# TensorE multiplies a constant block into an unread bank in eleven of its longer waits

## The reference: what is computed

```
mod = silu(c) @ w_ada + b_ada                      # shift, scale and gate of the two halves
mix = token_mixer(x * (1 + sc1) + sh1)             # w_in, sparse attention, a convolution, w_out
x   = layer_norm(ALPHA * x + g1 * mix)
ff  = (silu(h @ w_gate) * (h @ w_up)) @ w_down     # h = x * (1 + sc2) + sh2
x   = layer_norm(ALPHA * x + g2 * ff)
```

```
h = h + mixer(rms_norm(h))                         # w_in, recurrence or attention, w_out
h = h + swiglu(rms_norm(h))                        # 2816 hidden columns
h = h + sigmoid(rms_norm(h) @ w_gate) * (p @ w_proj)
```

## Time and profile before

| | us |
|---|---|
| median of 3 runs | 1235.39 (1232.58 to 1235.83) |
| the profiled execution, its own time | 1238.56 |
| its span, first to last instruction | 1236.7 |
| TensorE busy | 1087.3 (88%) |
| VectorE busy | 761.6 (62%) |
| ScalarE busy | 574.1 (46%) |
| GpSimd busy | 265.9 (21%) |
| mean granted TensorE clock | 0.926 |

### The profile page before, as it was taken

How to read it: one execution, slowest core, us unless ns; L and a number is a source line. 1 busy time by engine, 2 the same in 40 slices (tenths; PEclk the granted TensorE clock), 3 DMA queues, 4 the chain that set the end, 5 groups by cost and what they waited for, 6 DMA issues and landing times.

```text
span 1236.7 us, 20753 instructions
## 1 busy us (share of the span) xinstructions
PE 1087.3 (88%) x8097; PEld 1018.7 (82%) x8097; DVE 761.6 (62%) x1172; ACT 574.1 (46%) x963; POOL 265.9 (21%) x257
## 2 busy tenths in 40 slices
PE   1796646879999996989899999998998699999998
PEld 1786534869999985878799999998886499999997
DVE  5747876656655445775475665557676676555554
ACT  0544333455544335552364454465554655444452
POOL 0433232013332003020023332003120013333001
PEclk9897755889999998989899999998999899999999
DMA  8655453516553724341046554663334046553660
GB/s 314 212 203 185 156 203 136 168 37 206 202 182 113 216 75 173 132 173 68 1 162 210 174 180 141 187 235 140 137 136 136 1 137 204 203 169 110 196 207 36
DMA packets 188324, 193.45 MB, mean 156 GB/s; under 512 B 13721, under 2 KB 150722, under 8 KB 188130
## 3 DMA queue, kind: packets, MB, share of 16 engines
q1 hardware_dynamic: 184016, 179.88, 43.8%
q0 software_dynamic: 2640, 10.49, 2.3%
q10 hardware_dynamic: 1602, 2.18, 0.5%
HBM read 191.48 MB, written 1.05 MB: 156 GB/s over the span
## 4 chain that ended last, share of the span: by engine, by line
PE 66%; DVE 18%; ACT 6%; DMA 4%; issue 3%; POOL 1%; ACTq 1%; SPq 0%; POOLq 0%; DVEq 0%
PE gemm L1701 19%; PE gemm L1703 19%; PE gemm L1702 19%; DVE wlo L1152 5%; DMA raw<-in_w_in 3%; ACT whi L816 2%; DVE macc L1205 2%; PE aux L2013 1%; PE aux L1930 1%; DVE olo L1174 1%; DVE om L1423 1%; DVE xlo L1174 1%; DMA raw<-in_gla_w_in 1%; DMA raw<-in_w_ada 1%; DVE neg_max L1660 1%
## 5 line engine op out<-in xcount | busy, mean ns | idle before, releaser
L1701 PE MATMUL gemm<-ohi,whi 128*128 128x256 f32 x1536 | 442.2, 288 | 32.9 <-DVE wlo L1152 19.3
L1152 DVE TENSOR_TENSOR wlo<-raw,whi 128x1024 fp32r<-128x1024 f32 (+2 forms) x348 | 397.4, 1188 | 114.5 <-ACT whi L816 114.1
L1703 PE MATMUL gemm<-ohi,wlo 128*128 128x256 f32 x1536 | 437.0, 285 | 0.0
L1702 PE MATMUL gemm<-olo,whi 128*128 128x256 f32 x1536 | 436.4, 284 | 0.0
L816 ACT ACTIVATE whi<-raw 128x1024 fp32r<-128x1024 f32 (+2 forms) x348 | 309.2, 954 | 127.3 <-PE gemm L1703 100.8
L1701 PEld LDWEIGHTS gemm<-ohi,whi 128*128 128x128 f32 x1536 | 296.8, 193 | 40.4 <-DVE wlo L1152 22.3
L1702 PEld LDWEIGHTS gemm<-olo,whi 128*128 128x128 f32 x1536 | 297.4, 194 | 0.2
L1703 PEld LDWEIGHTS gemm<-ohi,wlo 128*128 128x128 f32 x1536 | 296.9, 193 | 0.0
L1701 PE MATMUL gemm<-acthi,whi 128*128 128x256 f32 x528 | 147.9, 280 | 0.0
L1703 PE MATMUL gemm<-acthi,wlo 128*128 128x256 f32 x528 | 147.6, 280 | 0.0
L1702 PE MATMUL gemm<-actlo,whi 128*128 128x256 f32 x528 | 147.3, 279 | 0.0
(11 more groups left out here) (306 smaller groups left out, 1488.2 us busy)
## 6 DMA issues: line engine op xcount, KB each, us to landing
raw<-in_ffn_w_in SPq DMA_DIRECT2D x44, 1024.0 KB, 6.8
raw<-in_ffn_w_out SPq DMA_DIRECT2D x32, 704.0 KB, 5.7
raw<-in_gla_w_in SPq DMA_DIRECT2D x6, 2048.0 KB, 7.8
raw<-in_diff_w_in SPq DMA_DIRECT2D x6, 2048.0 KB, 7.6
raw<-in_w_gate SPq DMA_DIRECT2D x11, 1024.0 KB, 5.1
raw<-in_w_up SPq DMA_DIRECT2D x11, 1024.0 KB, 7.5
raw<-in_w_down SPq DMA_DIRECT2D x16, 704.0 KB, 5.4
raw<-in_w_ada SPq DMA_DIRECT2D x5, 2048.0 KB, 8.0
```

The source lines that it names most:

```text
L1152: dve.tensor_tensor(wlo[hslot][:, q * w:(q + 1) * w], raw[slot][:, q * w:(q + 1) * w], whi[hslot][:, q * w:(q + 1) * w].bitcast(F32), ALU. ...
L1701: pe.matmul(dst, st_hi, mv_hi, start=start, stop=False)
L1702: pe.matmul(dst, st_hi, mv_lo, start=False, stop=False)
L1703: return pe.matmul(dst, st_lo, mv_hi, start=False, stop=stop_)
```

## The change

A helper issues n float32 matmuls of the block `ones` with a constant block into a bank whose content nobody reads. It has no semaphore of its own and is called at eleven places, one of them inside `layer_norm`, which runs twice. The moving block is 512 columns of `const`, but for the first place, where it is the 128 columns of `ones`. In all that is 13 matmuls of 128 columns and 37 of 512.

```
+            def keep_warm(bank, n, moving=None):
+
+                moving = const[:, 0:512] if moving is None else moving
+                banks.settle(bank)
+                for _ in range(n):
+                    pe.matmul(bank[:, 0:moving.shape[1]], ones[:, :], moving, start=True, stop=True)
...
             modulation(3)
+            keep_warm(G[2], 13, ones[:, :])
...
             gemm("in_hc", dve_read)
+            keep_warm(X[1], 3)
             modulation(5)
+            keep_warm(X[1], 4)
             gemm("in_gb", mixed_ready)
...
                 mean_sums(range(KT - 1, KT))
                 banks.claim(X[1], sd_ready)
+                keep_warm(X[2], 2)
                 for t in range(KT):
...
             STREAM = [banks.n[dve_read.name]]
+            keep_warm(X[2], 3)
             gemm("out0", dve_read, olo_from=8, order=(4, 5, 6, 7, 0, 1, 2, 3),
...
             layer_norm()
+            keep_warm(X[2], 4)
             ffn(0, False)
...
             layer_norm()
+            keep_warm(X[2], 4)
             start = next_operand()
...
-            gemm("gla_q", dve_read, after=lambda at, t: stats(tok=True) if t == 0 else None)
+            gemm("gla_q", dve_read, after=lambda at, t: (keep_warm(X[2], 4), stats(tok=True)) if t == 0 else None)
...
             gemm("gla_v", v_ready, shape="token")
+            keep_warm(X[2], 5)
             gemm("gla_r", r_ready)
...
             start = next_operand()
+            keep_warm(X[2], 2)
             gemm("out1", dve_read, olo_from=start, operand=(xhi, xlo))
...
             start = next_operand()
+            keep_warm(X[2], 4)
             gemm("out2", dve_read, olo_from=start, operand=(xhi, xlo))
```

## The result

The changed kernel takes 1222.46 us (median of four runs, 1219.69 to 1227.48) where the kernel before takes 1235.61 (four runs, 1232.58 to 1236.65): ratio 0.9895, 95% interval 0.9873 to 0.9917, a gain of 13.0 us. The forecast was 1229.5 with a range from 1225.0 to 1233.3; the sign was right, the size was not, and the time lies outside the range. The ratio is not the quotient of the two medians, and where executions scatter the two ways of reading a gain differ by up to 2 us. The changed kernel was timed twice more, on other chips, with gains of 12.1 and 10.9 us. The profiled execution took 1227.48 us, the slowest of the four, with a span of 1225.7 us and a mean granted clock of 0.951. That is 11.0 us less span than before.

What follows compares the result with a forecast made beforehand. TensorE, busy for 88% of the span and holding 66% of the chain that ended last, was taken as the bound. Gains of 1.3 + 3.9 + 1.4 + 2.5 = 9.1 us off the profiled 1238.56 gave 1229.5 us, range 1225 to 1233.3.

Steps and rivals of the forecast that it cites:

- steps 3, 4, 6 and 7: Kept clock gains 1.3 us in `out0`, 3.9 in both norms' sums of squares, 1.4 in `gla_q`, 2.5 in `gla_r`.
- Steps 1, 2, 5 and 8: `in_q`, `in_gb`, the first tiles behind the layer norms, `out1` and `out2`: a kept clock gives nothing.
- a gain of 5.9 us against the median, not 9.1: Whole kernel: timed runs missing norm falls already sit lower, so 1229.5 us is put on the changed kernel's median too.
- The first: Rival: idle time left before `out0` and `gla_r` still brings the fall, losing 3.8 us, 1233.3 us; chance 0.18.
- The second: Rival: the added matmuls, repeating one constant nobody reads, do not count as work; nothing changes, 1235.4 us; chance 0.06.
- The third: Rival: slow stretches in `in_q`, `in_gb`, behind the norms, `out1`, `out2` pay too, up to 4.5 us more, 1225 us; chance 0.10.
- its second form: Each slow stretch pays half its length, 14.2 us for six plus 3.9 for the norms, 1220.5 us; chance 0.01.
- The slower one: Rival: waits begin at 0.50, added matmuls delay `gla_q`, `out2`, `gla_r` and norms by 11.8 us, 1247 us; chance 0.04.

Runs made afterwards that it cites:

- e1_payers: The changed kernel with only the calls in `layer_norm`, before `out0`, in `gla_q` and before `gla_r` kept: 1228.18 us, ratio 0.9928.
- e7_late_rest: The changed kernel with only the four calls behind both layer norms and before `out1` and `out2` kept: 1236.76 us, ratio 0.9995.
- e14_payers_late: e1_payers plus the four calls behind both layer norms and before `out1` and `out2`: 1229.48 us, ratio 0.9938.
- e9_all_hold: The changed kernel, with GpSimd's last slab addition held until DVE has scaled the fourth head's probabilities: 1225.43 us, ratio 0.9911.
- e10_payers_hold: e1_payers, with GpSimd's last slab addition held until DVE has scaled the fourth head's probabilities: 1224.86 us, ratio 0.9903.
- e3_hold_pool: The kernel before, no added matmul, with GpSimd's last slab addition held until DVE has scaled the fourth head's probabilities: 1232.73 us, ratio 0.9957.
- e13_payers_tiny: e1_payers plus the three calls before `in_q` and around `modulation(5)`, their 20 matmuls cut to one column each: 1225.52 us, ratio 0.9905.
- e2_rest: The changed kernel with only the seven calls before `in_q`, around `modulation(5)`, behind both layer norms, before `out1` and `out2`: 1233.31 us, ratio 0.9969.
- e5_front: The changed kernel with only the three calls before `in_q` and around `modulation(5)` kept: 1236.74 us, ratio 0.9999.
- e11_norms: The changed kernel with only the call in `layer_norm` kept: 1235.8 us, ratio 0.9996.
- e6_front_tiny: The changed kernel with only the three calls before `in_q` and around `modulation(5)`, their 20 matmuls cut to one column each: 1236.5 us, ratio 0.9983.

## Why the prediction was wrong

**The sum of the clock's gains held.** 9.1 us were forecast for steps 3, 4, 6 and 7; e1_payers, which is just these, gave 8.9 (6.1 to 11.6 by its interval). That it comes so close is in part luck. The prices of a single fall were good where the calls took one away: 1.24 us in `out0` between the traces of before and after (1.3 forecast), 1.54 in `gla_q` (1.4), 2.7 in `gla_r` where the clock was kept (2.5), 1.66 in a norm (1.95, since 16 instructions take 3.72 us at the full clock and not 3.44). What the prediction lacked is how often a fall comes, and for how long. So the mean terms err in both directions: `out0` 0.5 instead of 1.3; the norms 1.7 and 1.1 instead of 1.95 each, since the second does not fall every time; `gla_q` 2.0 instead of 1.4, and another 0.8 in `gla_k` behind it; `gla_r` 1.4 instead of 2.5.

**Steps 1, 2, 5 and 8 were right: a kept clock there gives nothing.** e7_late_rest gave 0.6 us, e14_payers_late 1.2 less than e1_payers, and e9_all_hold, which has all eleven calls, 1.0 less than e10_payers_hold: nothing that can be told from zero. The Trainium skill ("TensorE: Matmul & The Clock Gate", Terms), by whose rule these stretches would have paid half their length, was not borne out: `out2` went from 0.50 to 1.00 and holds 18 matmuls in 4.10 us instead of 17.

**The first step that failed is the one in which the sum against the profiled execution became "a gain of 5.9 us against the median, not 9.1".** It assumed that typical executions miss falls and have less to win. Falls are missed, the second norm's in three of seven traces, the first norm's in none, but in the mean that takes 0.6 us off the gain, not 3.2, and e1_payers gave its 8.9 against the median. Nor do falls in the norms explain a profiled execution above its median: that of the changed kernel, with both norms at 3.73 us, stands 5.0 us above its own, and in the two repeats, with the same norms, 0.7 above and 0.3 below. Without this step the forecast would have been 1235.4 - 9.1 = 1226.3 us, inside the range and still 3.8 us above the measured time.

**The second is a term that is missing.** The prediction priced eleven places and treated the 80 us between `group_stats` and `out0` as rigid, so that whatever changes there stood at nothing, without a reason. It quoted no row from there. The collision of DVE and GpSimd at 190.69 stood in the trace of before, on the path to `out0`. It comes in all seven traces in which ACT finds its slab landed and GpSimd is not held; it comes in no trace in which ACT has to wait for the slab. It is worth 5.3 us alone (e3_hold_pool) and 2.8 to 3.1 us on top of the payers (e13_payers_tiny, e10_payers_hold); 8.9 and 3 make 12, between the 10.9 and the 13.0 of the three measurements. What moved it was not the clock, since one column does as well, but more TensorE instructions ahead of attention (40 in the changed kernel), with a code fetch that falls into the load of the last `w_ada` slab. That parting the two removes the collision is shown (e3_hold_pool). That the fetch is what delays the load is only inferred, from nineteen traces in which the two always come together; no run moved a fetch by itself.

**The rivals.** The first came half true: in `gla_r` the fall stayed, in six of the nine traces with five matmuls, for about 3.4 us; before `out0` it stayed in two of eleven (e9_all_hold, e10_payers_hold, `out0` 0.35 us longer) and in none of the changed kernel itself. The second, that the constant does not count as work, failed: the clock was kept. The third, that all slow stretches pay, gave nearly the measured time with 1225, and so did its second form with 1220.5, both for a reason that is false. The slower one did not happen: the waits still end with DVE, ACT or GpSimd, and no added matmul is late.

**What stays open.** How often the collision comes in executions without a profile: e2_rest gained 3.8 us with the same front calls with which e5_front, on another chip, gained 0.1, and their intervals do not meet, though both traces are free of the collision. Why the norms alone gave 0.5 us (e11_norms), where the traces give 2.8. And when the clock falls in `group_stats`, in the second norm and in `gla_k`.

## What to carry to other kernels

Price a kept clock only where the slowed matmuls set someone's start, count in how many traces the fall really comes, and take the sum off the median. Look for an instruction that takes many times as long as the same line does elsewhere (here 4.83 us and 0.55), and ask what ties its start to the other engine's. Where the tie hangs on a load that lands half a microsecond early, an edit upstream that only adds instructions can break it. And before crediting a whole change to its mechanism, time the half that ought to be worth nothing.

## What the hardware showed

- A 2 MB load landed after 11.3 to 11.6 us in the nine traces in which one packet of program code (0.02 MB on the instruction queue) falls into it, and after 10.2 to 10.5 in the ten others.
- Two DVE `tensor_scalar` instructions of 128x128 took 4.83 us beside one GpSimd addition of 128x2048 that began with them, and 0.55 us where they began 0.7 us before it.
- A wait of about 2 us on TensorE was followed by the lower clock in all seven traces at the first norm and in only four of seven at the second. At `group_stats` it was kept behind a wait of 3.11 us (e5_front) and fell behind one of 1.89 (e6_front_tiny). In e1_payers' `gla_k` the clock fell to 0.58 with TensorE busy for all of the 3.00 us.
- 26 float32 instructions of 128 columns took 4.52 us at a granted clock of 1.00, 0.35 us for one matmul of two, where half the 256-column price was 0.215.
